# Second model's kernel on one core: paired matmuls in the feed-forward stages, GpSimd's share of low parts in the mixers, the order of the norm and of the first mixture's copies

## The chip, the cores and the metric

The kernel runs on one core of a Trainium2 chip. The metric is the device time of one execution in microseconds, the median of several runs; less is better. The engines are TensorE (PE in the profile, its weight loads PEld), VectorE (DVE), ScalarE (ACT), GpSimd (POOL) and SyncE (SP, which issues the loads of weights).

## The reference

One batch of 256 tokens, 1024 wide, goes through two chained models, all in float32:

```python
def first_block(x, mem, ...):            # two layers
    for layer in range(2):
        if layer == 0: mix = gla_layer_mixer(h, mem, ...)   # gated linear attention + memory attention
        else:          mix = sb_layer_mixer(h, mem, ...)    # stick-breaking attention + memory attention
        h = layer_norm(ALPHA * h + mix)
        h = layer_norm(ALPHA * h + peer(h, ...))            # 16384 experts, top 16 in each of 8 heads
    return h

def gla_layer_mixer(x, ...):
    q, k, v, r, glr, qm = jnp.split(x @ w_in, A_IN_SPLITS, axis=-1)
    log_g = log_sigmoid(glr @ w_gate2 + b_gate) / 16
    o = gla_chunked(q * 64 ** -0.5, k, v, log_g)            # 6 heads, chunks of 64 tokens
    o = o * rsqrt(mean(o * o) + EPS) * head_g
    o = o * silu(r)
    return concatenate([o, memory_attention(qm, mem, w_mem_kv)]) @ w_out

def second_block(x, ...):                # two layers
    for l in range(2):
        x = x + 0.5 * swiglu(rms_norm(x), w_gate, w_up, w_down)      # (silu(h wg) * (h wu)) wd, 2816 wide
        na, df, gq, dl = split(rms_norm(x) @ w_in)          # 4 heads each, with norms and rotations
        o = [neighborhood(na), diff(df), gqa_axial(gq), dilated(dl)]  # diff: (p0 - lam * p1) v, then rms_norm
        x = x + concatenate(o) @ w_out
        x = x + 0.5 * swiglu(rms_norm(x), w_gate, w_up, w_down)
```

## The kernel before

**Products.** Every weight is read once from memory, as 933 units of 512 KB, in the order of use. A unit has two halves of 128 x 512; a half is split into a high part WH (rounded to the fast float32 form, ScalarE, `split`, L1152) and a low part WL = RAW - WH (VectorE at L1758, or GpSimd at L2562 where `low_on_pool(j)` says so: every fourth half, j % 4 == 3, but for some stretches). Activations are split likewise, XTh and XTl. A product is three matmuls: high x high, low x high, high x low, all recorded at L475 (`mm`). The halves pass through five slots (NHALF), the raw units through four (NRAW). ScalarE makes the high part of half j + 5 once TensorE has used half j (`spent`).

**Two forms of product.** In `Tensor.cols` (L498) the weights are the stationary operand and 256 tokens move: 12 matmuls of 256 columns for a half. In `Tensor.depth` (L555) the activations stand, the weights move, 512 columns in each matmul, 2 blocks of tokens x 3 = 6 matmuls for a half, summed in the banks 0 to 3.

**Stages.** Ten stages: gated linear attention (37 units), PEER (272), stick breaking (28), PEER (272), feed forward (66), mixer (30), feed forward, feed forward (66 each), mixer (30), feed forward (66). In the profile of before the first runs to about 159 us, the PEERs to 999 and from 1141 to 1982, the first mixer of the second model from 2186 to 2346, the second from 2732 to 2892.

**Feed forward.** 22 steps over f: gate and up (`cols`, two halves each, both in one bank, 4 + f % 4, gate in its first 256 columns and up in its last), then the product of hidden unit f - 2 (`depth`). The hidden chain of f runs beside it: VectorE multiplies the gate part by the norm's factor (GR, L2408), ScalarE takes Silu (L1620), VectorE multiplies by up (HID, L2412), ScalarE makes the high part FH (L1624), VectorE the low part FL (L2414).

**The order around it.** Each engine's program is written out by one Python class (Tensor, Scalar, Vector, Gpsimd, Sync) with the same stage functions. What does not belong to the stream of halves is a generator in a `Pace`: each half is one `tick`, which adds `rate` to a credit and steps the background list `bg` while there is credit, and each generator of the foreground list `fg` once. `until(name)` steps until a name is reached, foreground first. In a mixer the background is the four attentions (na, df, gq, dl), and between df and gq the norm of difference attention, `od`. The queues are in order on each engine: a background instruction stands where the ticks put it. ScalarE's `halves(n)` does n ticks with a `split` behind each; the copy of a finished bank out of PSUM comes behind that (L1420, L1430 in the first mixture, L1486 in stick breaking, L1544 in PEER). Attention: VectorE's row maximum of a head (L1994), ScalarE's exponentials (L1291), transposes on TensorE, ScalarE's copy of them (L1300), products with the values, VectorE's output (L2022 and others). L2485 to L2490 with L1777 to L1790 are VectorE's part of `od`, L2451 and L2457 the norms of the queries and keys, L2500 and L1681 copies out of the input product, L2434 to L2440 rotations, L1976 the low part of the output product's activations.

## Time and profile before

| | before |
|---|---|
| median of three runs | 3088.6 us (3087.66 to 3089.96) |
| the profiled execution | 3092.74 us, of it 3090.5 us span |
| TensorE matmul | 3000.8 us (97%), 21828 instructions |
| VectorE | 2109.8 us (68%) |
| ScalarE | 1628.2 us (53%) |
| GpSimd | 469.1 us (15%), 363 instructions |
| TensorE's mean granted clock | 0.983 of full |

The span is the time from the first to the last recorded instruction of the profiled execution; its own time is 2.24 us longer. A matmul's row shows its start exactly and its end by a model, so the time that one costs in a stream is the distance to the next start, not its length. The idle time ahead of an instruction stands in brackets, with what ended it. The granted clock says which share of the full 2.4 GHz TensorE had in a stretch: 0.50 is 1.2 GHz.

### The profile page before, as it was taken

To read this page: it belongs to the slowest core of one execution; us is meant where nothing else is said; L and a number is where in the kernel's file an instruction comes from. 1 tells how busy PE (TensorE), PEld (TensorE's weight loads), DVE (VectorE), ACT (ScalarE), POOL (GpSimd) and SP (SyncE) were. 2 spreads that over 40 slices of the span, in tenths; PEclk is the share of its full clock that TensorE was granted. 3 is DMA by queue.
4 is the path that set the end of the run, shared out by engine and by line. 5 is a ranking of instruction groups with operands and counts; after the bars stand their busy time and mean duration, and the time that the engine had idled before them with its cause. 6 is when DMAs were issued, how large, how long until landed. Compare 5 with 4: busy or idle time off the path is not lost.

```text
span 3090.5 us, 56441 instructions
## 1 busy us (share of the span) xinstructions
PE 3000.8 (97%) x21828; PEld 2712.4 (88%) x21828; DVE 2109.8 (68%) x4512; ACT 1628.2 (53%) x3157; POOL 469.1 (15%) x363
## 2 busy tenths in 40 slices
PE   8989999999999989999999999899989999998999
PEld 8789999988887879999998888799868999987898
DVE  4559978799755555997879965655765565566555
ACT  5445544454555555554444455555655555565554
POOL 1212200000022112220000012123101222311122
PEclk9999999999999999999999999999999999999999
DMA  6345554454555335554454555465423556542354
GB/s 216 121 144 182 181 175 161 158 170 164 191 191 177 127 100 174 178 186 163 160 166 163 167 198 191 153 219 185 152 75 132 189 176 214 185 162 76 130 184 157
DMA packets 138363, 509.47 MB, mean 165 GB/s; under 512 B 15329, under 2 KB 15858, under 8 KB 136818
## 3 DMA queue, kind: packets, MB, share of 16 engines
q1 hardware_dynamic: 134352, 489.22, 48.0%
q10 hardware_dynamic: 3746, 16.65, 1.5%
q8 instruction: 174, 2.85, 0.4%
q14 instruction: 91, 0.75, 0.1%
HBM read 504.76 MB, written 1.05 MB: 164 GB/s over the span
## 4 chain that ended last, share of the span: by engine, by line
PE 89%; DVE 6%; ACT 3%; issue 1%; DMA 0%; POOL 0%; ACTq 0%; DVEq 0%
PE ps L475 88%; PE ps L479 1%; ACT WH L1152 1%; DVE WL L1758 1%; ACT BIG L1291 1%; DVE XTl L1830 0%; DVE BIG L1994 0%; DVE BIG L1799 0%; DVE BIG L2500 0%; DVE BIG L1847 0%; DMA BIG<-in_memT 0%; DVE BIG L1989 0%; DVE BIG L2451 0%; DVE H L1924 0%; DVE BIG L1855 0%
## 5 line engine op out<-in xcount | busy, mean ns | idle before, releaser
L1152 ACT ACTIVATE WH<-RAW 128x512 fp32r<-128x512 f32 x1866 | 1158.4, 630 | 1082.1 <-PE ps L475 1068.7
L1758 DVE TENSOR_TENSOR WL<-RAW,WH 128x512 fp32r<-128x512 f32 x1537 | 1102.7, 725 | 710.1 <-ACT WH L1152 698.8
L475 PE MATMUL ps<-XTh,WH 128*128 128x256 f32 x3928 | 1128.4, 287 | 19.8 <-DVE XTl L1807 8.7
L475 PE MATMUL ps<-XTl,WH 128*128 128x256 f32 x3928 | 1118.4, 285 | 0.0
L475 PE MATMUL ps<-XTh,WL 128*128 128x256 f32 x3928 | 1118.0, 285 | 0.0
L2562 POOL TENSOR_TENSOR WL<-RAW,WH 128x512 fp32r<-128x512 f32 x329 | 440.5, 1339 | 2593.6 <-ACT WH L1152 2593.6
L475 PEld LDWEIGHTS ps<-XTh,WH 128*128 128x128 f32 x3928 | 760.2, 194 | 28.6 <-issue 9.8
L475 PEld LDWEIGHTS ps<-XTl,WH 128*128 128x128 f32 x3928 | 760.8, 194 | 2.9
L475 PEld LDWEIGHTS ps<-XTh,WL 128*128 128x128 f32 x3928 | 760.2, 194 | 0.0
L475 PE MATMUL ps<-WH,GH 128*128 128x512 f32 x1056 | 420.2, 398 | 6.5 <-DVE BIG L2435 2.0
L475 PE MATMUL ps<-WH,GL 128*128 128x512 f32 x1056 | 413.7, 392 | 0.0
L475 PE MATMUL ps<-WL,GH 128*128 128x512 f32 x1056 | 413.5, 392 | 0.0
L475 PEld LDWEIGHTS ps<-WH,GH 128*128 128x128 f32 x1056 | 199.0, 188 | 48.0 <-issue 6.2
L475 PEld LDWEIGHTS ps<-WH,GL 128*128 128x128 f32 x1056 | 199.3, 189 | 42.1
L475 PE MATMUL ps<-WH,HIDR 128*128 128x512 f32 x704 | 233.8, 392 | 1.2 <-POOL WL L2562 1.2
L475 PEld LDWEIGHTS ps<-WL,GH 128*128 128x128 f32 x1056 | 199.4, 189 | 39.1
L475 PE MATMUL ps<-BIG 128*128 128x64 f32 (+6 forms) x966 | 157.3, 313 | 16.9 <-ACT BIG L1291 8.2
L475 PEld LDWEIGHTS ps<-BIG 128*128 128x128 f32 (+4 forms) x966 | 126.8, 192 | 43.2 <-issue 12.8
L475 PE MATMUL ps<-WH,XTh 128*128 128x512 f32 (+1 forms) x400 | 158.4, 396 | 1.1 <-ACT BIG L1420 1.1
L475 PEld LDWEIGHTS ps<-WH,HIDR 128*128 128x128 f32 x704 | 132.6, 188 | 29.1 <-POOL WL L2562 2.9
L475 PE MATMUL ps<-WH,XTl 128*128 128x512 f32 (+1 forms) x400 | 150.0, 375 | 0.0
L475 PE MATMUL ps<-WL,XTh 128*128 128x512 f32 (+1 forms) x400 | 149.6, 374 | 0.0
(197 smaller groups left out, 2590.7 us busy)
## 6 DMA issues: line engine op xcount, KB each, us to landing
RAW<-in_w SPq DMA_DIRECT2D x933, 512.0 KB, 3.3
BIG<-in_ln ACTq DMA_DIRECT2D x4, 1024.0 KB, 7.8
BIG<-in_sk ACTq DMA_DIRECT2D x2, 1024.0 KB, 5.1
BIG<-in_na_bias ACTq DMA_DIRECT2D x2, 1024.0 KB, 5.0
BIG<-in_qk_gain ACTq DMA_DIRECT2D x2, 960.0 KB, 5.8
BIG<-in_memT ACTq DMA_DIRECT2D x4, 256.0 KB, 7.6
BIG<-in_xT ACTq DMA_DIRECT2D x1, 1024.0 KB, 5.3
H<-in_x ACTq DMA_DIRECT2D x1, 1024.0 KB, 8.1
```

The source lines that it names most:

```text
L475: return self.e.matmul(out, lhsT, rhs, start=start, stop=stop, skip_group_check=loose)
L479: return self.e.transpose(out, in_, self.c.IDENT[0:n, 0:n])
L1152: e.activation(wh, raw, ACT.Copy).then_inc(*c.hi.mark(j))
L1291: e.activation(t.E[:, i % 3, w], src[:, w], ACT.Exp, bias=s[:, blk:blk + 1], accum_out=s[:, 2 + blk:3 + blk]).then_inc(*c.exps.mark(tag, i ...
L1758: e.tensor_tensor(wl, raw, wh.bitcast(F32), ALU.subtract).then_inc(*c.lo_v.mark(j))
L2562: e.tensor_tensor(wl, raw, wh.bitcast(F32), ALU.subtract).then_inc(*c.lo_p.mark(j))
```

## The change

It has six parts.

1. `low_on_pool`: inside a mixer, from the 16th half to four before the end, every second half's low part is GpSimd's, not every fourth.
2. The norm `od` is appended to the foreground when difference attention is done, no longer an item of the background between df and gq; `until` takes the background first unless it is `od` that is wanted; chunk 2 of the output product waits for it.
3. XTh and XTl are the halves of one tile XT of 512 columns. Gate and up of f from 2 on are made by `wide_cols`: WH by [XTh | XTl] in one matmul of 512 columns, WL by XTh in one of 256. The two parts of the result stand beside each other and have to be added: ScalarE copies the second (PARTS), VectorE adds it. Gate and up have a bank each, 6 and 7 or 4 and 5 in turn.
4. `depth`, where it starts a sum, takes token block 1 first and waits for each bank apart, no longer for all four ahead.
5. ScalarE's `halves` takes a function for the copy of the finished bank, and issues it ahead of the last tick and high part.
6. The first mixture: the scores of a pair of heads wait for that pair's q and k alone; the root of each pair's norm is taken by itself; the first gating is made early; the Silu of the gate is taken in the copy out of PSUM, with its table loaded ahead.

```diff
+    if any(BASE[stage] + 16 <= j < BASE[stage + 1] - 4 for stage in MIX):
+        return j % 2 == 1
     return j % 4 == 3
...
     def until(self, name):
         while name not in self.reached:
-            q = self.fg or self.bg
+            q = self.bg if self.bg and name[1] != "od" else self.fg or self.bg
             self.step(q[0], q)
...
+        self.XT = sb("XT", [P, 8, 512], FR)
+        self.XTh, self.XTl = self.XT[:, :, 0:256], self.XT[:, :, 256:512]
...
+    def wide_cols(self, key, ps):
+        c = self.c
+        for half in range(2):
+            j, wh, wl = self.half(key)
+            parts = blocks(4)
+            for a in range(4):
+                self.mm(ps[:, :], wh[:, parts[a]], c.XT[:, half * 4 + a, :], half + a == 0, half * 4 + a == 7, loose=True)
+            for a in range(4):
+                t = self.mm(ps[:, 0:256], wl[:, parts[a]], c.XTh[:, half * 4 + a, :], False, half * 4 + a == 7, loose=True)
+            t.then_inc(*c.used.mark(j))
+            self.pace.tick()
...
     def depth(self, key, ah, al, first):
-            for blk in range(2):
-                t = self.three(c.B[blk * 2 + half][:, :], ah[:, TB[blk]], al[:, TB[blk]], wh, wl, first, False)
+            for blk in (1, 0) if first else (0, 1):
+                out = c.B[blk * 2 + half]
+                if first:
+                    out = self.bank(blk * 2 + half)
+                t = self.three(out[:, :], ah[:, TB[blk]], al[:, TB[blk]], wh, wl, first, False)
...
     def inner(self):                       # Tensor, first mixture
         for p in range(3):
-            e.wait_ge(*c.vec.at("ke"))
+            e.wait_ge(*c.vec.at("qe", p))
...
     def ffn_stage(self, layer, which):     # Tensor
-            ps = self.bank(4 + f % 4)
-            self.cols(("fg", layer, which, f), ps[:, 0:256], stage if f == 0 else None)
-            self.cols(("fu", layer, which, f), ps[:, 256:512])
-            self.empty[4 + f % 4] = c.vec.at(stage, "hid", f)
+            if f < 2:
+                ps = self.bank(4 + f)
+                self.cols(("fg", layer, which, f), ps[:, 0:256], stage if f == 0 else None)
+                self.cols(("fu", layer, which, f), ps[:, 256:512])
+                self.empty[4 + f] = c.vec.at(stage, "hid", f)
+            else:
+                for b, key in zip((6, 7) if f % 2 == 0 else (4, 5), ("fg", "fu")):
+                    self.wide_cols((key, layer, which, f), self.bank(b))
+                    self.empty[b] = c.vec.at(stage, "hid", f)
...
     def halves(self, n, done=None):        # Scalar
-        for _ in range(n):
+        for k in range(n):
             self.j += 1
+            if done and k == n - 1:
+                self.e.wait_ge(*self.c.used.at(self.j - 1))
+                done()
             self.pace.tick()
             self.split()
...
     def hidden(f):                         # Scalar
+            if f >= 2:
+                for k, ps in enumerate(c.ffn_banks(f)):
+                    e.wait_ge(*c.used.at(BASE[stage] + 4 * f + 2 * (f - 2) + 1 + 2 * k))
+                    if f >= 4:
+                        e.wait_ge(*c.vec.at(stage, "hid", f - 2))
+                    e.activation(t.PARTS[:, 2 * r + k, :], ps[:, 256:512], ACT.Copy).then_inc(*c.act.mark(stage, "parts", f, k))
...
     def hidden(f):                         # Vector
+                e.wait_ge(*c.act.at(stage, "parts", f, 0))
+                e.tensor_tensor(t.GR[:, r, :], gate[:, 0:256], t.PARTS[:, 2 * r, :], ALU.add).then_inc(*c.vec.mark())
+                self.own()
+                e.tensor_tensor(t.GR[:, r, :], t.GR[:, r, :], c.RB, ALU.mult).then_inc(*c.vec.mark(stage, "gr", f))
+                e.wait_ge(*c.act.at(stage, "parts", f, 1))
+                e.tensor_tensor(t.UP[:, r, :], up[:, 0:256], t.PARTS[:, 2 * r + 1, :], ALU.add).then_inc(*c.vec.mark("up", stage, f))
+                up = t.UP[:, r, :]
+                self.own()
...
     def attend(self, stage, name, k):      # and on each other engine
         yield from self.attention(...)
+        if name == "df":
+            self.pace.fg.append(self.od(stage))
...
     def gla_stage(self):                   # Scalar
-        e.wait_ge(*c.vec.at("sum", 2))
-        self.rsqrt(t.rs[:, 0:12], 1.0 / 128, c.EPS5, ..., "rsum")
-        e.activation(t.vr[:, :, 1024:1536], t.vr[:, :, 1024:1536], ACT.Silu).then_inc(*c.act.mark("silu", 1))
         e.preload_act_table_set(TABLES)
+        self.gla_root(2)
```

TensorE in a feed-forward stage of the second model, one half of gate, up and the hidden product, before. ps6 and so on are the PSUM banks, HIDR holds the hidden unit's parts:

```order
L475 MATMUL ps6<-XTh,WH 128x256
L475 MATMUL ps6<-XTl,WH 128x256
L475 MATMUL ps6<-XTh,WL 128x256
L475 MATMUL ps6<-XTh,WH 128x256
L475 MATMUL ps6<-XTl,WH 128x256
L475 MATMUL ps6<-XTh,WL 128x256
L475 MATMUL ps0<-WH,HIDR 128x512
L475 MATMUL ps0<-WL,HIDR 128x512
L475 MATMUL ps0<-WH,HIDR 128x512
L475 MATMUL ps2<-WH,HIDR 128x512
L475 MATMUL ps2<-WL,HIDR 128x512
L475 MATMUL ps2<-WH,HIDR 128x512
```

The same place, changed, from gate and up of one f to the hidden product:

```order
L486 MATMUL ps6<-XT,WH 128x512 x4
L486 MATMUL ps6<-XT,WL 128x256 x4
L486 MATMUL ps6<-XT,WH 128x512 x4
L486 MATMUL ps6<-XT,WL 128x256 x4
L486 MATMUL ps7<-XT,WH 128x512 x4
L486 MATMUL ps7<-XT,WL 128x256 x4
L486 MATMUL ps7<-XT,WH 128x512 x4
L486 MATMUL ps7<-XT,WL 128x256 x4
L486 MATMUL ps2<-WH,HIDR 128x512
L486 MATMUL ps2<-WL,HIDR 128x512
```

A triple of 256 columns has become a matmul of 512 columns and one of 256; the low parts WL now come last in a half, gate and up stand in two banks.

VectorE in the first mixer of the second model, behind the input product's last copies (L2500), before. ps4 and ps5 are the scores of two heads:

```order
L2500 SCALAR_TENSOR_TENSOR BIG<-ps1,BIG 128x512
L2485 TENSOR_REDUCE BIG<-BIG 128x8
L1777 TENSOR_SCALAR BIG<-BIG,CST 128x8
L1784 TENSOR_TENSOR BIG<-BIG 128x8
L1786 TENSOR_TENSOR BIG<-BIG 128x8
L1788 TENSOR_SCALAR BIG<-BIG 128x8
L1790 TENSOR_TENSOR BIG<-BIG 128x8
L2490 TENSOR_TENSOR BIG<-BIG 128x2x256
L2451 TENSOR_REDUCE BIG<-BIG 128x16
L1976 TENSOR_TENSOR GL<-ps6,GH 128x512
L1994 TENSOR_REDUCE BIG<-ps4 128x2
L1994 TENSOR_REDUCE BIG<-ps5 128x2
```

Changed (L2576 is L2500, L2041 is L1994, L2560 is L2485, L2524 is L2451):

```order
L2576 SCALAR_TENSOR_TENSOR BIG<-ps1,BIG 128x512
L2041 TENSOR_REDUCE BIG<-ps4 128x2
L2041 TENSOR_REDUCE BIG<-ps5 128x2
L2524 TENSOR_REDUCE BIG<-BIG 128x16
L2023 TENSOR_TENSOR GL<-ps6,GH 128x512
L2560 TENSOR_REDUCE BIG<-BIG 128x8
L1824 TENSOR_SCALAR BIG<-BIG,CST 128x8
L2041 TENSOR_REDUCE BIG<-ps4 128x2
L2041 TENSOR_REDUCE BIG<-ps5 128x2
```

The two maxima stood behind the norm and the reduction L2451; now they come first, and the norm is spread behind them.

ScalarE at the end of the first mixture, before. ps0 and ps1 are the input product's last banks, L1170 and L1172 the norm's root, L1443 the gate's Silu:

```order
L1152 ACTIVATE WH<-RAW 128x512 x3
L1430 ACTIVATE BIG<-ps0 128x512
L1430 ACTIVATE BIG<-ps1 128x512
L1170 ACTIVATE BIG<-BIG,CST 128x12
L1172 ACTIVATE BIG<-BIG 128x12
L1443 ACT_TABLE_LOAD
L1443 ACTIVATE BIG<-BIG 128x2x512
L1444 ACT_TABLE_LOAD
L1152 ACTIVATE WH<-RAW 128x512 x2
```

Changed (L1471 is L1430, L1179 is L1152, L1201 and L1203 are the root of the last pair):

```order
L1422 ACT_TABLE_LOAD
L1422 ACTIVATE BIG<-CST 128x1
L1309 ACTIVATE GH<-ps6 128x512
L1179 ACTIVATE WH<-RAW 128x512 x2
L1471 ACTIVATE BIG<-ps0 128x512
L1471 ACTIVATE BIG<-ps1 128x512
L1179 ACTIVATE WH<-RAW 128x512
L1485 ACT_TABLE_LOAD
L1201 ACTIVATE BIG<-BIG,CST 128x4
L1203 ACTIVATE BIG<-BIG 128x4
L1179 ACTIVATE WH<-RAW 128x512 x2
```

The Silu table is loaded ahead, the pass over 1024 columns is gone, and the copies of ps0 and ps1 come behind two high parts instead of three.

## Rows read from the trace of the kernel before

**Rows 1.** The page: busy us and share of an engine; the chain that ended last.

```profile
PE 3000.8 (97%) x21828; PEld 2712.4 (88%) x21828; DVE 2109.8 (68%) x4512; ACT 1628.2 (53%) x3157; POOL 469.1 (15%) x363
...
PE 89%; DVE 6%; ACT 3%; issue 1%; DMA 0%; POOL 0%; ACTq 0%; DVEq 0%
```

**Rows 2.** Table by windows: length, busy us of each engine (count), granted clock, DMA.

```profile
2186.00:2346.00 160.00, 147.12 (x766) 117.11 (x765) 99.29 (x224) 87.98 (x226) 19.08 (x14) 0.95 0.29 99
2354.00:2531.00 177.00, 176.69 (x1266) 167.01 (x1265) 99.36 (x173) 93.52 (x175) 40.11 (x32) 1.00 0.56 184
```

**Rows 3.** Timeline of TensorE, feed forward: start, length, [idle before <-what ended it].

```profile
2018.20 0.28 PE L475 MATMUL ps<-XTh,WH 128*128 128x256 f32 x1
...
2023.96 0.40 PE L475 MATMUL ps<-WH,HIDR 128*128 128x512 f32 x1
...
2026.70 0.28 PE L475 MATMUL ps<-XTh,WH 128*128 128x256 f32 x1
```

**Rows 4.** Timeline of VectorE, feed forward, the hidden chain.

```profile
2455.89 0.42 DVE L2408 TENSOR_TENSOR BIG<-ps,BIG 128x256 f32<-128x256 f32 x1
2456.85 0.42 DVE L2412 TENSOR_TENSOR BIG<-BIG,ps 128x256 f32<-128x256 f32 x1 [0.55 <-ACT BIG L1620]
```

**Rows 5.** Timeline of ScalarE, the same stretch.

```profile
2457.31 0.42 ACT L1624 ACTIVATE HIDR<-BIG 128x256 fp32r<-128x256 f32 x1 [0.56 <-DVE BIG L2412]
2457.63 1.73 ACT L1152 ACTIVATE WH<-RAW 128x512 fp32r<-128x512 f32 x3
```

**Rows 6.** Timeline of GpSimd, the same stretch.

```profile
2458.33 1.30 POOL L2562 TENSOR_TENSOR WL<-RAW,WH 128x512 fp32r<-128x512 f32 x1 [6.09 <-ACT WH L1152]
```

**Rows 7.** Timeline of TensorE, the same stretch: the low part's first use.

```profile
2461.65 0.28 PE L475 MATMUL ps<-XTh,WL 128*128 128x256 f32 x1
```

**Rows 8.** The tile RAW: duration of its readers in ns, min/median/max.

```profile
L1758 DVE TENSOR_TENSOR WL<-RAW,WH x1537: 661/692/1787, 6.3 to 3080.7; 128x512 fp32r<-128x512 f32 x193
...
L2562 POOL TENSOR_TENSOR WL<-RAW,WH x329: 1265/1297/2277, 11.2 to 3076.3; 128x512 fp32r<-128x512 f32 x165
```

**Rows 9.** Timeline of VectorE, first mixer of the second model.

```profile
2281.95 1.40 DVE L2500 SCALAR_TENSOR_TENSOR BIG<-ps,BIG 128x512 f32<-128x512 f32 x2
2283.27 0.67 DVE L2485 TENSOR_REDUCE BIG<-BIG 128x8 f32<-128x512 f32 x1
...
2287.70 1.28 DVE L1994 TENSOR_REDUCE BIG<-ps 128x2 f32<-128x512 f32 x2
```

**Rows 10.** Timeline of TensorE, first mixer of the second model.

```profile
2283.61 1.99 PE L475 MATMUL ps<-BIG 64*128 64x256 f32 x8
2289.48 2.07 PE L475 MATMUL ps<-BIG 64*128 64x256 f32 x4 [3.88 <-ACT BIG L1291]
...
2302.03 0.70 PE L475 MATMUL ps<-WH,GH 128*128 128x512 f32 x1 [0.98 <-DVE BIG L2435]
```

**Rows 11.** Timeline of ScalarE, the same stretch.

```profile
2288.41 0.47 ACT L1291 ACTIVATE BIG<-ps,BIG 128x256 f32<-128x256 f32 x1 [2.89 <-DVE BIG L1994]
```

**Rows 12.** TensorE's waits, 2186 to 2346: us in total, times, longest.

```profile
PE ps L479 <- ACT BIG L1300: 3.7, 4, 2.2
```

**Rows 13.** Table by windows as in rows 2, of stretches at half clock.

```profile
134.60:138.00 3.40, 3.40 (x9) 2.54 (x9) 1.79 (x5) 3.36 (x4) 0.00 (x0) 0.51 0.47 154
2288.50:2295.30 6.80, 5.82 (x21) 4.65 (x21) 2.60 (x8) 3.79 (x16) 0.00 (x0) 0.50 0.18 68
```

**Rows 14.** Timelines of TensorE in the first model: first mixture, PEER, stick breaking.

```profile
76.98 0.50 PE L475 MATMUL ps<-WH,XTh 128*128 128x512 f32 x1 [1.05 <-ACT BIG L1420]
...
106.55 1.53 PE L475 MATMUL ps<-BIG 64*128 64x256 f32 x6 [0.44 <-issue]
...
133.65 0.47 PE L475 MATMUL ps<-WH,GH 128*128 128x512 f32 x1 [1.90 <-ACT BIG L1170]
...
220.13 3.06 PE L475 MATMUL ps<-BIG 128*128 128x128 f32 x25 [1.05 <-ACT BIG L1544]
...
1109.19 0.47 PE L475 MATMUL ps<-WH,GH 128*128 128x512 f32 x1 [1.52 <-ACT BIG L1486]
```

149 lines of the change are left out of this document (84 added, 65 removed).

## The prediction, made before the change was run

> **What bounds the kernel now.** I read the page's busy shares and its chain first. TensorE is busy 97% of the span, and 89% of the chain that ended last is TensorE [rows 1]: time is saved only where TensorE issues less, stops waiting, or gets its clock back. The table by stage comes next, to see where it is not full: a feed-forward stage fills 176.69 of 177 us of its steady part, a mixer 147.12 of 160 us at a granted clock of 0.95 [rows 2]. So a feed-forward stage can be shortened by cheaper matmuls alone, a mixer by its waits.
>
> In the feed-forward stage I read the starts of TensorE's rows, since ends are modelled. From the first product with XTh at 2018.20 to the first hidden product at 2023.96 lie 48 matmuls of 256 columns, 0.120 us each; from there to 2026.70 lie 12 of 512 columns, 0.228 us each [rows 3]. One iteration over f is 5.76 + 2.74 = 8.50 us.
>
> **The change part by part.**
>
> *Paired matmuls.* A half now costs 12 × 0.120 = 1.44 us. Changed, it is 4 matmuls of 512 columns and 4 of 256: 4 × 0.228 + 4 × 0.120 = 1.392 us, 0.048 less. Halves of gate and up with f of at least 2: 4 × 20 × 4 stages = 320. That is **−15.4 us**. A pitch of 0.226 would make it −17.9, one of 0.230 −12.8; I take 0.228, since it is measured beside the 256-column stream itself. These columns are charged at full clock, where the stages run [rows 2].
>
> TensorE's saving is only real if nothing else becomes late. ScalarE gains two copies of 256 columns in each f, VectorE two additions. Today the hidden unit's chain runs: gate × RB on VectorE at 2455.89, product at 2456.85 [rows 4], high part on ScalarE at 2457.31, and only then three high parts of weights at 2457.63, which had queued behind it [rows 5]. The first of them feeds the GpSimd low part at 2458.33, done at 2459.63 [rows 6]; the half that uses it sends its first low product at 2461.65 [rows 7]. The slack is 2.0 us. The chain grows by VectorE's addition ahead of gate × RB (0.42 us), and by what the second copy pushes the Silu back, about as much: some 0.8 us. That is within the slack, and the new order of a half gives 0.9 us more, since its low products come behind four matmuls of 512 columns. Cost taken: 0. Its cover is those 2.0 us; the bound above them is rival D. Below nothing it cannot go: no wait stands in this place to be won.
>
> The banks of gate and up are used again two iterations later instead of four; the product that frees them runs at 2456.85 [rows 4], some 0.8 us later then, and their next use is over 8 us behind that: nothing waits there.
>
> *Pool's share.* The order gives GpSimd ten more low parts in each mixer, and VectorE ten fewer. On VectorE that is 10 × 0.692 = 6.9 us less, on GpSimd 10 × 1.297 = 13.0 us more [rows 8]. For a waiting product a GpSimd low comes 0.6 us later than VectorE's, and NHALF = 5 slots of lead cover that, as they did in the half above (2.0 us). In the queue of VectorE, which is what the attentions wait for, it is a gain, but one that is spread. I put it at 0 by itself, ±1 us for each mixer.
>
> The same medians have a tail: VectorE's low takes up to 1.787 us and GpSimd's up to 2.277 [rows 8]. The Trainium skill, page "SBUF — State Buffer", section "🔬 SBUF: two separate sides", says that GpSimd and a VectorE operation with two SBUF inputs take their shared port as an exclusive lock, so that the other fully blocks; the tails agree with it. By that rule the ten moved lows per mixer could give back as much VectorE time as they free, and the sum would lose what the mixers gain; this is rival E.
>
> *Norm of difference attention, and the order in the queues.* Ahead of TensorE's longest wait in the mixer, ScalarE's exponentials wait for VectorE's two maxima at 2287.70. Those stand behind the norm (L2485 at 2283.27 and what follows it) and another reduction (L2451), which come right behind the two of L2500 [rows 9]. TensorE makes the scores from 2283.61 on, and next does something at 2289.48, 3.88 us idle [rows 10]. In the changed order both maxima follow the two copies of L2500, and the norm comes behind them. The scores of the first head are four of eight matmuls in 1.99 us, so there at 2284.6; maximum 0.64 us to 2285.3; two exponentials, 1.07 us as now (2288.41 [rows 11] to 2289.48): TensorE goes on at about 2286.4, 3.0 us earlier. What is late next is the same chain for the later heads, and the first output product at 2302.03, which waits 0.98 us on VectorE [rows 10]. Less VectorE work ahead of it gives another 1 us. **−4 us for each mixer, −8 us.** The wait of chunk 2 of the output product for the norm costs nothing: the norm's last step is done tens of instructions ahead of it. Bounds: −1 (the gap only moves to the waits on L1300, now 3.7 us in four [rows 12]) and −10 (below).
>
> *The clock.* Behind each long gap comes a stretch at half clock: 2288.5 to 2295.3 runs at 0.50, TensorE busy for 5.82 of 6.80 us [rows 13], so it holds some 3 us that could be saved. I take no gain of it, because waits like those on L1300 (the longest 2.2 us) remain.
>
> *First mixture (GLA).* ScalarE's copy of a finished bank comes ahead of the next high part instead of behind it (0.58 us each: three in 1.73 [rows 5]): of TensorE's 1.05 us at 76.98 some 0.5 goes. Scores need one pair of q and k, not all three: of the idle time ahead of 106.55 (0.44, and the matmul's slow start) up to 0.6. The gap of 1.90 us at 133.65 [rows 14] is the two copies of 512 columns plus one high part ahead of them; bank by bank, and with the roots and the first gating done earlier, it goes: −2.0, the start of its first matmul with it. The half-clock stretch behind it (134.6 to 138.0, TensorE busy in all of 3.40 us [rows 13]) would go with the gap: −1.7. Sum **−4.8 us**; at worst nothing, if the gating on VectorE is late in its place. ScalarE loads as many tables as before.
>
> *The other copies.* Stick-breaking mixer, 1.52 us at 1109.19: the last bank's copy comes ahead of a high part and long before the gap: −1.5. Query stage of PEER, 1.05 at 220.13: −0.5, twice [rows 14]. **−2.6 us.**
>
> **Sum.** −15.4 − 8 − 4.8 − 2.6 = −30.8 us. Against the profiled execution's own 3092.74 us (span 3090.5 and 2.24 around it) that is 3061.9. This execution is 4.1 above the median of the three, 3088.6, so for the median I say **3057.8 us**.
>
> **Rivals.**
>
> *B, the pair saves nothing.* If a matmul is charged by columns alone, a 512-column one costs two of 256, 0.240 us, and 15.4 us of the sum go: 3073.2 us. For it: the columns streamed are the same. Against it: 0.228 stands in the trace beside 0.120 [rows 3]. The Trainium skill, page "TensorE: Matmul & The Clock Gate", section "Back-to-back issue gap", gives an isolated gap of N/2.4 + 2.5 ns, by which a pair saves only 2.5 ns, or an estimated 3.2 us over 1280 pairs; the trace's pitch of 0.120 us for 256 columns differs from it, and the measurement decides.
>
> *C, the mixers' half-clock stretches go too.* With the gap of 3.88 us closed, two of the stretches [rows 13] fall away, 3 us each, in both mixers: −12 more, 3045.8 us. For it: the stretches begin only behind gaps. Against it: the waits on L1300 stay.
>
> *D, slower: the longer hidden chain takes all slack.* VectorE waits in order for ScalarE's copies, and ScalarE's high parts are queued behind the Silu. If all four added operations lie in series, with two handshakes of 0.55 us as ahead of the product [rows 4], the chain grows by 4 × 0.42 + 2 × 0.55 = 2.8 us; less the 2.0 of slack TensorE waits 0.8 us in each of 80 iterations, +64 us: 3122 us. It decides from a growth of 2.0 us on, and eats the whole gain from 2.4 us. Against it: the first copy runs beside the up product's matmuls and the up addition beside the Silu.
>
> *E, the ten moved lows collide.* A colliding low costs VectorE up to 1.1 us more (1.787 against 0.692), so ten of them free nothing, and the mixers' queues are as late as now: the 8 us go, 3065.8 us. For it: the tails [rows 8], and mixers whose VectorE works on SBUF alone in long operations. Against it: only 14 GpSimd operations in 160 us today [rows 2].
>
> *F, the change does little of what it says,* the gaps in first mixture, mixers and PEER being set by something else, and the pairs eaten by waits: about 3086 us. The order shows the pairs and the moved maxima, so this is small.
>
> **How the numbers follow.** Forecast A 0.55, B 0.10, C 0.18, D 0.04, E 0.09, F 0.04. Two tenths of a per cent, 6.2 us, is what a measurement of this kernel can tell from no change. A, B, C and E are faster: 0.92; F the same: 0.04; D slower: 0.04. The range reaches down to C with a pair's upper bound (3045.8 − 2.5, some rounding down: 3042), and up to B, or to A without the mixers' 8, the first mixture's 4.8 and 2.6 of the pairs (3073.2): 3074. D and F are left out, and the tails of the others.
>
> **What would show it.** In the changed profile: 512-column products of XT and WH starting 0.228 us apart and an iteration of 8.31 us (8.50 − 4 × 0.048); TensorE busy in all of a feed-forward stage, its waits under 1 us each; ScalarE's high parts queued behind the hidden chain no later than 2.0 us. A mixer with the gap of 3.88 us down to about 1 and 156 us long; half clock still in two or three stretches. No gap at the start of the first mixture's output product. The prediction is wrong if high or low parts of weights release TensorE in the feed-forward stages (D), if pairs start 0.240 apart (B), or if mixers keep 160 us.

## The result and the profile after

The changed kernel takes 3069.2 us, the median of six runs (3065.61 to 3071.44), against 3088.13 (3087.41 to 3089.96) for the kernel before: 18.9 us less, a ratio of 0.9936 with a 95% interval of 0.9924 to 0.9949. Forecast were 3057.8 us within 3042 to 3074. The sign and the range held; of the 30.8 us that the sum promised, 12 did not come.

The page of the changed kernel, its busy times and its chain, answers to [rows 1]. Lines have moved: L486 is L475, L1179 is L1152, L1805 is L1758, L2637 is L2562.

```profile
PE 2984.5 (97%) x20548; PEld 2637.2 (86%) x20548; DVE 2183.1 (71%) x4666; ACT 1666.0 (54%) x3321; POOL 499.2 (16%) x383
...
PE 87%; DVE 7%; ACT 4%; issue 1%; DMA 0%; POOL 0%; ACTq 0%; DVEq 0%
```

There are 1280 matmuls fewer, 20 operations more on GpSimd, 154 more on VectorE, and TensorE still bounds the whole: its share of the chain fell by 2 points, VectorE's and ScalarE's rose by one each.

The table by windows of the changed kernel, one row for each stage, cut at TensorE's last product of the stage (length, TensorE's busy us, granted clock, DMA share, GB/s):

```profile
0.00:161.30 161.30, 146.90 (x852) 0.99 0.48 165
161.30:1000.50 839.20, 830.23 (x6615) 0.99 0.54 174
1000.50:1140.50 140.00, 130.21 (x865) 0.95 0.35 115
1140.50:1980.10 839.60, 831.10 (x6615) 0.99 0.54 174
1980.10:2182.30 202.20, 191.78 (x1028) 0.97 0.56 185
2182.30:2337.50 155.20, 145.25 (x768) 0.97 0.32 102
2337.50:2528.80 191.30, 189.09 (x1020) 0.99 0.56 182
2528.80:2720.20 191.40, 189.12 (x1019) 0.99 0.59 195
2720.20:2874.60 154.40, 143.68 (x767) 0.98 0.31 103
2874.60:3063.60 189.00, 186.83 (x1012) 1.00 0.55 173
```

The same cuts in both traces, in us, with the time that each stage spent at half clock (the cuts are read to 0.01 us here and rounded, so a length can differ by 0.1 from a row's):

| stage | before | after | difference | forecast | half clock before, after |
|---|---|---|---|---|---|
| first mixture | 158.9 | 161.3 | +2.4 | -4.8 | 3.4, 3.4 |
| PEER | 840.2 | 839.2 | -1.0 | -0.5 | 13.7, 10.2 |
| stick breaking | 141.9 | 140.0 | -1.9 | -1.5 | 13.7, 13.7 |
| PEER | 840.6 | 839.6 | -1.0 | -0.5 | 13.7, 13.7 |
| feed forward | 204.2 | 202.2 | -2.0 | -3.85 | 13.7, 13.7 |
| mixer | 160.5 | 155.2 | -5.3 | -4 | 17.1, 10.2 |
| feed forward | 193.3 | 191.3 | -2.0 | -3.85 | 3.4, 3.4 |
| feed forward | 191.9 | 191.4 | -0.5 | -3.85 | 0, 3.4 |
| mixer | 160.7 | 154.4 | -6.3 | -4 | 17.1, 6.8 |
| feed forward | 192.4 | 188.9 | -3.5 | -3.85 | 3.4, 0 |

The differences sum to -21.1 us, as do the spans (3090.5 to 3069.4). Two places are off: the pairs gave half of what was forecast, and the first mixture became longer. The mixers gave 3.6 us more. The profiled execution took 3071.28 us, 2.1 above the median of the six, and its mixers hold more half clock than others of the same code: in a kernel below whose mixers are not edited (the gating behind the pair's low part) they take 153.2 and 153.8 us, with 3.4 us at half clock in each.

**The pairs, in the trace.** TensorE's timeline of the changed kernel in a feed-forward stage, one iteration from its first product with XT to the hidden product:

```profile
2447.01 1.07 PE L486 MATMUL ps<-XT,WH 128*128 128x512 f32 x4
2447.92 0.64 PE L486 MATMUL ps<-XT,WL 128*128 128x256 f32 x4
2448.39 1.09 PE L486 MATMUL ps<-XT,WH 128*128 128x512 f32 x4
2449.32 0.63 PE L486 MATMUL ps<-XT,WL 128*128 128x256 f32 x4
...
2452.60 0.40 PE L486 MATMUL ps<-WH,HIDR 128*128 128x512 f32 x1
```

Four of 512 columns take 0.91 to 0.93 us from the first start to the next group's (0.2325 each in the second and later halves, not 0.228), four of 256 take 0.47 (0.118, not 0.120). The four halves take 2452.60 - 2447.01 = 5.59 us, against 5.76 [rows 3]. The hidden product's twelve take 2.77 us on the mean of this stage, against 2.74. An iteration is 8.35 us long, not the 8.31 of the forecast, and was 8.50: 0.15 saved, 0.19 forecast.

The hidden chain, VectorE and then ScalarE, answers to [rows 4, 5]. L2475 and L2479 are the two additions, L2477 the product with the norm's factor, L2485 the hidden unit, L1661 the two copies:

```profile
2445.78 0.42 DVE L2475 TENSOR_TENSOR BIG<-ps,BIG 128x256 f32<-128x256 f32 x1
2446.23 0.42 DVE L2477 TENSOR_TENSOR BIG<-BIG 128x256 f32<-128x256 f32 x1
2446.57 0.42 DVE L2479 TENSOR_TENSOR BIG<-ps,BIG 128x256 f32<-128x256 f32 x1
2447.24 0.43 DVE L2485 TENSOR_TENSOR BIG<-BIG 128x256 f32<-128x256 f32 x1 [0.25 <-ACT BIG L1665]
```

```profile
2445.04 0.64 ACT L1661 ACTIVATE BIG<-ps 128x256 f32<-128x256 f32 x2
...
2448.02 1.66 ACT L1179 ACTIVATE WH<-RAW 128x512 fp32r<-128x512 f32 x3
```

and GpSimd, which answers to [rows 6]:

```profile
2448.71 1.30 POOL L2637 TENSOR_TENSOR WL<-RAW,WH 128x512 fp32r<-128x512 f32 x1 [5.95 <-ACT WH L1179]
```

Counted from the start of the hidden product (2454.35 before, 2444.24 now), HID starts 3.0 us behind it where it was 2.5, and the three queued high parts start at 3.78 where they were at 3.28: the chain grew by 0.5 us. That is inside the slack of 2.0: the GpSimd low behind the first of them is done at 2450.01, and TensorE first uses it at 2452.13, 2.1 us later. TensorE waits nowhere in the steady iterations.

**The mixer, in the trace.** VectorE and then TensorE of the changed kernel, answering to [rows 9, 10]; L2576 is L2500, L2041 is L1994, the maxima:

```profile
2279.52 1.41 DVE L2576 SCALAR_TENSOR_TENSOR BIG<-ps,BIG 128x512 f32<-128x512 f32 x2
2280.84 1.28 DVE L2041 TENSOR_REDUCE BIG<-ps 128x2 f32<-128x512 f32 x2
```

```profile
2279.30 1.99 PE L486 MATMUL ps<-BIG 64*128 64x256 f32 x8
...
2283.24 1.13 PE L486 MATMUL ps<-BIG 64*128 64x256 f32 x4
...
2291.36 0.66 PE L490 MATMUL ps<-CST,BIG 128*128 128x128 f32 x4 [1.29 <-ACT BIG L1331]
...
2296.65 0.47 PE L486 MATMUL ps<-WH,GH 128*128 128x512 f32 x1 [0.48 <-ACT BIG L1735]
```

From the first scores to the output product were 2302.03 - 2283.61 = 18.4 us; now 2296.65 - 2279.30 = 17.35. From the first scores to the third head's were 5.87, now 3.94; the idle 3.88 us ahead of it are gone. These two distances understate the gain, because the changed order puts other products there: TensorE makes 96 matmuls between the first scores and the output product, where it made 68. The 69th of them starts 18.4 us behind the first before and 13.0 us now. What was late next is ScalarE's copy of transposes (1.29 us at 2291.36). The output product runs its first six matmuls at full clock, where they were at half: they start 0.23 us apart, not 0.43.

### The profile page after: what moved, and what is told of

The parts are those of the page before. It is cut to its first block, busy times and chain, and to the rows that moved or that the text cites. A ratio compares the mean times of both kernels' runs of the same rounds, so it can differ in the third digit from the quotient of the medians.

```text
span 3069.4 us, 54436 instructions
## 1 busy us (share of the span) xinstructions
PE 2984.5 (97%) x20548; PEld 2637.2 (86%) x20548; DVE 2183.1 (71%) x4666; ACT 1666.0 (54%) x3321; POOL 499.2 (16%) x383
## 3 DMA queue, kind: packets, MB, share of 16 engines
HBM read 504.76 MB, written 1.05 MB: 165 GB/s over the span
## 4 chain that ended last, share of the span: by engine, by line
PE 87%; DVE 7%; ACT 4%; issue 1%; DMA 0%; POOL 0%; ACTq 0%; DVEq 0%
PE ps L486 86%; PE ps L490 1%; ACT WH L1179 1%; DVE WL L1805 1%; ACT BIG L1322 1%; DVE BIG L2041 0%; DVE XT L1877 0%; DVE BIG L1846 0%; DVE BIG L2576 0%; DVE BIG L1894 0%; DMA BIG<-in_memT 0%; DVE BIG L2036 0%; DVE BIG L2530 0%; DVE BIG L2485 0%; DVE H L1971 0%
## 5 line engine op out<-in xcount | busy, mean ns | idle before, releaser
L1179 ACT ACTIVATE WH<-RAW 128x512 fp32r<-128x512 f32 x1866 | 1152.4, 629 | 998.2 <-PE ps L486 986.9
L1805 DVE TENSOR_TENSOR WL<-RAW,WH 128x512 fp32r<-128x512 f32 x1517 | 1100.8, 735 | 647.4 <-ACT WH L1179 639.0
L486 PE MATMUL ps<-XT,WH 128*128 128x256 f32 (+1 forms) x6576 | 1327.7, 308 | 20.2 <-DVE XT L1854 8.7
L486 PEld LDWEIGHTS ps<-XT,WH 128*128 128x128 f32 x6576 | 1059.1, 193 | 60.8 <-issue 9.9
L486 PE MATMUL ps<-XT,WL 128*128 128x256 f32 x3928 | 957.6, 283 | 0.0
L2637 POOL TENSOR_TENSOR WL<-RAW,WH 128x512 fp32r<-128x512 f32 x349 | 470.1, 1347 | 2538.7 <-ACT WH L1179 2538.7
L486 PEld LDWEIGHTS ps<-XT,WL 128*128 128x128 f32 x3928 | 710.0, 192 | 26.8
L486 PE MATMUL ps<-WH,GH 128*128 128x512 f32 x1056 | 418.9, 397 | 2.6 <-DVE GL L2412 1.0
L486 PE MATMUL ps<-WH,GL 128*128 128x512 f32 x1056 | 411.8, 390 | 0.0
L486 PE MATMUL ps<-WL,GH 128*128 128x512 f32 x1056 | 411.6, 390 | 0.0
L486 PE MATMUL ps<-WH,XT 128*128 128x512 f32 (+1 forms) x800 | 255.3, 386 | 3.9 <-DVE XT L2023 3.4
L486 PE MATMUL ps<-WH,HIDR 128*128 128x512 f32 x704 | 236.0, 395 | 2.2 <-POOL WL L2637 1.8
L486 PEld LDWEIGHTS ps<-WH,GH 128*128 128x128 f32 x1056 | 198.3, 188 | 44.3 <-DVE GL L2412 2.8
L486 PEld LDWEIGHTS ps<-WH,GL 128*128 128x128 f32 x1056 | 198.2, 188 | 42.1
L486 PEld LDWEIGHTS ps<-WL,GH 128*128 128x128 f32 x1056 | 198.6, 188 | 38.8
L486 PEld LDWEIGHTS ps<-WH,XT 128*128 128x128 f32 x800 | 148.9, 192 | 36.6 <-issue 8.0
L486 PE MATMUL ps<-BIG 128*128 128x64 f32 (+6 forms) x966 | 155.5, 311 | 8.0 <-DVE BIG L2258 2.1
L486 PEld LDWEIGHTS ps<-WH,HIDR 128*128 128x128 f32 x704 | 132.2, 188 | 32.4 <-POOL WL L2637 3.5
L486 PEld LDWEIGHTS ps<-BIG 128*128 128x128 f32 (+4 forms) x966 | 125.6, 191 | 33.3 <-issue 12.8
L486 PE MATMUL ps<-WL,XT 128*128 128x512 f32 (+1 forms) x400 | 149.7, 374 | 0.0
L486 PE MATMUL ps<-WL,HIDR 128*128 128x512 f32 x352 | 138.4, 393 | 0.0
L2412 DVE TENSOR_TENSOR GL<-BIG,GH 128x256 fp32r<-128x256 f32 x256 | 107.4, 420 | 0.2
```

The lines of the kernel that those rows point to most:

```text
L486: return self.e.matmul(out, lhsT, rhs, start=start, stop=stop, skip_group_check=loose)
L1179: e.activation(wh, raw, ACT.Copy).then_inc(*c.hi.mark(j))
L1805: e.tensor_tensor(wl, raw, wh.bitcast(F32), ALU.subtract).then_inc(*c.lo_v.mark(j))
L2412: e.tensor_tensor(c.GL[:, r, :], c.peer.G[:, g, :], c.GH[:, r, :].bitcast(F32), ALU.subtract).then_inc(*c.xtl.mark(stage, "g", g))
L2637: e.tensor_tensor(wl, raw, wh.bitcast(F32), ALU.subtract).then_inc(*c.lo_p.mark(j))
```

## Experiments

Each edit is to the changed kernel, unless it says otherwise. Comparisons with the kernel before are with its runs beside it, 3087.6 to 3090.2 us in the median.

### Pairs undone, and pairs alone

```diff
-                for b, key in zip((6, 7) if f % 2 == 0 else (4, 5), ("fg", "fu")):
-                    self.wide_cols((key, layer, which, f), self.bank(b))
+            self.cols(("fg", layer, which, f), ps[:, 0:256], stage if f == 0 else None)
+            self.cols(("fu", layer, which, f), ps[:, 256:512])
```

> The changed kernel with gate and up made by matmuls of 256 columns again, in one bank for each f, without the two copies and two additions of each hidden unit; all else as changed. Theory (the pairs save what the starts show, 8.50 us an iteration before and 8.35 changed, less 0.8 us of new waits in each feed-forward stage): this run is slower than the changed kernel by 80 x 0.15 - 4 x 0.8 = 9 us, about 3078 us, with iterations of 8.50 us. Rival B (columns are all that is paid, and the stages became shorter by the earlier copies and banks): within 2 us of the changed kernel.

Measured: 3074.4 us (3073.95 to 3078.94), ratio to before 0.9955 (0.9938 to 0.9972), 5.2 us slower than the changed kernel. Its feed-forward stages are those of the kernel before again: 204.2, 193.3, 192.0 and 192.5 us. Rival B is out. But 5.2 is less than the 9 of the theory, and the runs of either kernel spread by 5 us, much of it with the granted clock. The two executions of each kernel with a mean clock of 0.990 lie 8 us apart (3073.95 and 3073.96, against 3065.61 and 3066.22). The stages, below, give the same size.

The other way round, to the kernel before, the pairs and with them the waits bank by bank in `depth` (and in PEER, where four waits ahead of the sum go):

> The kernel before with the pairs alone: gate and up by matmuls of 512 and 256 columns with their copies, additions and banks, and the sum's banks waited for one by one. Theory: 0.147 us less for each of 80 iterations, 0.8 us of new waits in each of four stages: 8 to 9 us faster than before, 3079 to 3080 us. Rival (the gain needs the other parts, or what the table by stage shows is partly their work): 3084 us or more.

Measured: 3073.2 us (3071.02 to 3073.53), ratio 0.9948 (0.9932 to 0.9965), 14.8 us less than before, more than expected. The stages show why. Stick breaking is 1.7 us shorter and the mixers are 2.0 and 4.0 us shorter in this kernel, and none of them has a pair. In stick breaking that is `depth` starting its sum bank by bank: the 1.52 us ahead of the output product [rows 14] are gone from this trace, and stand unchanged in the one with the norm's order alone. In the mixers `depth` is the one edited part that they use, but half clock fell too, from 17.1 us to 13.7 and 10.2, and how the gain divides is not shown. A feed-forward stage without half clock is 189.9 us long here, 192.0 in the kernel without pairs. The row by windows of the third such stage, with the pairs alone:

```profile
2529.60:2719.60 190.00, 187.74 (x1020) 160.77 (x1019) 133.31 (x245) 114.94 (x248) 55.14 (x45) 1.00 0.61 197
```

and with the pairs undone:

```profile
2532.90:2724.80 191.90, 189.91 (x1339) 177.83 (x1338) 113.94 (x204) 105.35 (x207) 54.57 (x45) 1.00 0.60 195
```

So the pairs are worth 2.0 us in a stage, both at full clock, 8 in all. The steady iterations give 20 x 0.15 = 3.0 of it; 0.8 to 1.0 us go at the two ends of the stage, where the hidden chain has no slack: by the starts, some 0.15 us at the first hidden product, where TensorE waits 0.45 us on a GpSimd low instead of 0.30, 0.33 in the turn after it and 0.36 ahead of the last products.

### The order of lengths

```diff
             for a in range(4):
                 self.mm(ps[:, :], wh[:, parts[a]], c.XT[:, half * 4 + a, :], ...)
-            for a in range(4):
                 t = self.mm(ps[:, 0:256], wl[:, parts[a]], c.XTh[:, half * 4 + a, :], ...)
```

> The changed kernel with a half of gate and up in alternating order: WH by 512 columns, WL by 256, four times, no longer four of one and four of the other. The starts in the changed kernel are 0.232 us apart for 512 columns and 0.118 for 256, where I had 0.228 and 0.120. Theory A (the cost is one for each matmul, of whatever length, and the order of lengths does not matter): the iteration stays at 8.35 us and the time within 1 us. Theory B (runs of one length, or loads of weights that come nearer together in the 256-column run, cost something): the iteration falls to 8.31 us, 3 us less in all. Rival C (each change of length costs): 8.4 us or more, 4 us slower or worse.

Measured: 3066.3 us (3065.59 to 3068.31), no more than 3 us from the changed kernel, within both spreads. The trace is sharper. Two hidden products that follow each other start 8.39 us apart:

```profile
2442.20 0.40 PE L486 MATMUL ps<-WH,HIDR 128*128 128x512 f32 x1
...
2450.59 0.40 PE L486 MATMUL ps<-WH,HIDR 128*128 128x512 f32 x1
```

and the two stages without half clock take 190.4 and 190.5 us, where the next kernel below has 189.8 and 189.9. A half has eight changes of length, not two, and costs 0.01 us more. Theories A and B are wrong. Rival C is right in kind, that changes of length cost, and wrong in its price of 4 us: the iterations sum to some 3 us, and the whole shows none of it. In this order a 512-column matmul starts 0.236 us ahead of its successor, a 256-column one 0.117 (medians). What makes the pitch of one depend on its neighbours stays open.

### GpSimd's share in the mixers

```diff
-    if any(BASE[stage] + 16 <= j < BASE[stage + 1] - 4 for stage in MIX):
-        return j % 2 == 1
```

> The changed kernel with the old rule for GpSimd's low parts (every fourth half) in the mixers of the second model; all else as changed. Theory (most of the 5.3 and 6.3 us that a mixer gained come from the order of the maxima and the norm): the mixers lose about 1 us each and the run is 1 to 3 us slower than the changed kernel. Rival (freeing VectorE of ten low parts made the gain): a mixer is 4 us longer, the run 8 us slower. Rival E (moved lows collide and give back what they free): no difference or faster by 1 to 2 us.

Measured: 3067.1 us (3063.12 to 3073.01), ratio 0.9931 (0.9914 to 0.9948). The mixers by windows (TensorE, its loads, VectorE, ScalarE, GpSimd):

```profile
2183.40:2337.50 154.10, 144.12 (x767) 114.46 (x766) 100.82 (x226) 88.20 (x227) 18.82 (x14) 0.98 0.32 103
2717.20:2871.70 154.50, 145.24 (x768) 115.39 (x767) 100.26 (x226) 88.28 (x228) 18.79 (x14) 0.97 0.32 103
```

In the changed kernel, with the larger share:

```profile
2182.30:2337.50 155.20, 145.25 (x768) 115.26 (x766) 95.85 (x216) 88.22 (x227) 33.35 (x24) 0.97 0.32 102
2720.20:2874.60 154.40, 143.68 (x767) 114.51 (x766) 96.41 (x216) 88.19 (x227) 33.29 (x24) 0.98 0.31 103
```

GpSimd's larger share takes 5.0 and 3.9 us off VectorE and nothing off the stage; neither the theory's 1 us nor the rival's 4 us for each mixer came. The ten lows alone took 6.7 us off VectorE. Its 179 other operations are the same in both kernels, and with the larger share they take 1.3 and 2.5 us longer in sum (79.4 against 78.1, and 80.1 against 77.6): the three products of 1024 columns in the first mixer take 1.59 us on the mean, not 1.22. That is rival E's collision, at a part of its price.

### The norm's place

```diff
+        pace.bg.insert(2, self.od(stage, layer))
...
-        if name == "df":
-            self.pace.fg.append(self.od(stage, layer))
```

> The changed kernel with the norm of difference attention back in the background between df and gq, and the old rule of what a wait for a name steps first; all else as changed, GpSimd's share too. Theory (the order of the maxima is the gain): the gap of 3.9 us ahead of the first scores of gq is back, with its half clock, and each mixer is 4 to 5 us longer: 8 to 10 us slower than the changed kernel. Rival (GpSimd's share is the gain): within 2 us of it.

Measured: 3076.9 us (3075.39 to 3079.54), ratio 0.9966 (0.9953 to 0.9978), 7.7 us slower than the changed kernel; the mixers take 158.9 and 158.4 us. The gap is back, in TensorE's timeline:

```profile
2284.32 2.07 PE L485 MATMUL ps<-BIG 64*128 64x256 f32 x4 [3.90 <-ACT BIG L1320]
```

And alone, put into the kernel before:

> The kernel before with the norm of difference attention in the foreground and the new rule of waiting for a name, nothing else. Theory: the maxima come ahead of the norm, the gap of 3.9 us ahead of the scores closes, and each mixer is 4.5 us shorter plus what half clock goes with it, 9 to 12 us in all: 3077 to 3080 us. Rival (it works only with the ten lows moved to GpSimd): under 5 us.

Measured: 3075.7 us (3073.24 to 3079.28), ratio 0.9958 (0.9944 to 0.9972), 12.3 us less than before. Each mixer is 153.8 us long, 6.8 less, at a clock of 0.99:

```profile
2185.90:2339.80 153.90, 142.61 (x768) 112.84 (x766) 100.85 (x227) 88.42 (x228) 18.73 (x14) 0.99 0.32 103
```

The order alone gives the whole gain in the mixers, with GpSimd's old share. By the same count of matmuls in both traces, this kernel is 4.3 us ahead directly behind where the gap stood, 5.9 us ahead 60 matmuls later and 6.7 to 6.9 at the stage's end; half clock fell from 17.1 us to 3.4 in each mixer. The gains do not add: the pairs' kernel, with `depth` bank by bank, gave 2.0 and 4.0, the norm alone 6.7 and 6.9, both together 5.3 and 6.3 in the profiled execution, with 10.2 and 6.8 us of half clock, and 7.4 and 6.9 in the one with 3.4 us in each. So what all other parts add in the mixers once the norm is moved is 0.7 us at most.

### The first mixture

The changed trace shows the stage 1.5 us ahead of the kernel before at its output product (132.15 against 133.65 [rows 14]) and 2.4 us behind at its end. That it is longer is no accident of one execution: in the five traces whose first mixture is the changed kernel's (this one and the runs without pairs, with a quarter for GpSimd, with the norm in the back and alternating) it ends at 159.7 to 162.0 us, in the two whose first mixture is that of the kernel before at 158.9. From the output product's first start to its last are 29.0 to 30.4 us in the five and 25.3 in the two. TensorE waits inside the product:

```profile
132.15 0.50 PE L486 MATMUL ps<-WH,GH 128*128 128x512 f32 x1 [0.56 <-DVE GL L2023]
137.46 0.50 PE L486 MATMUL ps<-WH,GH 128*128 128x512 f32 x1 [0.34 <-DVE WL L1805]
142.50 0.55 PE L486 MATMUL ps<-WH,XT 128*128 128x512 f32 x1 [3.38 <-DVE XT L2023]
```

VectorE's queue up to the low part of XT that it waits for (L1831 to L1837 are a root's last steps, L2178 and L2182 the gating of the next pair):

```profile
137.94 1.25 DVE L1831 TENSOR_TENSOR BIG<-BIG 128x4 f32<-128x4 f32 x1
...
139.82 0.69 DVE L2178 TENSOR_TENSOR BIG<-BIG 128x512 f32<-128x512 f32 x1
140.55 0.69 DVE L2182 TENSOR_TENSOR BIG<-BIG 128x512 f32<-128x512 f32 x1
...
141.76 0.68 DVE L2023 TENSOR_TENSOR XT<-ps,XT 128x512 fp32r<-128x512 f32 x1
```

and GpSimd beside it:

```profile
137.31 1.86 POOL L2637 TENSOR_TENSOR WL<-RAW,WH 128x512 fp32r<-128x512 f32 x1 [0.52 <-ACT WH L1179]
```

ScalarE's high part of that XT was there at 138.2. Three things stand between: an operation on four columns that takes 1.25 us, where its like takes 0.16, and ends when GpSimd's low does (139.19 and 139.17); the root's steps; and the next pair's gating. First the order:

```diff
         def early(ch):
-            if ch < 4:
-                self.gla_root(ch // 2 + 1)
-                self.gated_heads(ch // 2 + 1)
+            if ch > 0:
+                self.gla_root(ch // 2)
+                self.gated_heads(ch // 2)
```

> The changed kernel with one thing moved on VectorE: in the first mixture the root and the gating of heads 2 and 3 (and then 4 and 5) come behind the low part of the pair before them, as in the kernel before; the first gating stays early. Theory (the gap of 3.4 us on TensorE ahead of the first product with XT at 142.5 is VectorE's order, the low part of XT waits behind the next gating): the gap shrinks to under 1 us, the half clock behind it goes, and the run is 3 to 5 us faster than the changed kernel, 3064 to 3066 us. Rival (the roots pair by pair themselves, with a handshake for each, are what is late): the gap moves to the next pair and the time stays within 1 us.

Measured: 3067.8 us (3066.3 to 3071.16), 1.4 us from the changed kernel, within the spread. The first mixture ends at 161.1 us, not 161.3. What the rival foretold came: the wait moved.

```profile
140.24 0.50 PE L486 MATMUL ps<-WH,XT 128*128 128x512 f32 x1 [1.26 <-DVE XT L2023]
144.53 0.66 PE L490 MATMUL ps<-CST,BIG 128*128 128x128 f32 x4 [1.27 <-DVE BIG L2182]
152.65 0.66 PE L490 MATMUL ps<-CST,BIG 128*128 128x128 f32 x4 [2.00 <-DVE BIG L2182]
```

Now each gating is waited for, and one operation of each lies beside a GpSimd low (the second one runs from 150.05 to 151.33):

```profile
142.82 1.65 DVE L2182 TENSOR_TENSOR BIG<-BIG 128x512 f32<-128x512 f32 x1
...
150.10 1.77 DVE L2178 TENSOR_TENSOR BIG<-BIG 128x512 f32<-128x512 f32 x1
```

```profile
142.65 1.28 POOL L2637 TENSOR_TENSOR WL<-RAW,WH 128x512 fp32r<-128x512 f32 x1 [3.61 <-ACT WH L1179]
```

So the lows were taken from GpSimd, to that order:

```diff
-    return j % 4 == 3
+    return j % 4 == 3 and j not in (63, 67, 71)
```

> The run with the gating behind the pair's low part, and three lows of the first mixture's output product (the 16th to 18th that GpSimd makes) on VectorE. Theory (what lengthened the output product from 23.4 to some 27.5 us is, beside the order, VectorE operations of 0.16 and 0.69 us that last 1.25 to 1.77 us while a GpSimd low runs, and four small root operations of 0.75 us ahead of each gating): without the GpSimd lows the gatings last 0.69 us each and the product is 2 us shorter, 25 to 26 us, though VectorE has three lows more. Rival (VectorE is simply full there, collisions or not): no shorter than with the gating moved alone.

Measured: 3067.3 us (3064.75 to 3068.82); the output product takes 26.6 us, where it took 29.1 (from the first matmul's start to the last's; 25.3 in the kernel before). The theory had 25 to 26. The rival is out: VectorE has three lows more and the product is shorter all the same. The roots' place instead, GpSimd's lows kept:

```diff
+            if ch > 0:
+                self.gated_heads(ch // 2)
             if ch < 4:
                 self.gla_root(ch // 2 + 1)
-                self.gated_heads(ch // 2 + 1)
```

> The run with the gating behind the pair's low part, and each root's four small operations one place earlier, behind the gating before it, ahead of the pair's low part; GpSimd's lows as changed. Theory: the gatings of the second and third pair no longer have 0.75 us ahead of them, the waits of TensorE on the gating (1.27 and 2.00 us) shrink by 0.75 each, 1 to 1.5 us off the output product. Rival (the first low part is late by as much): the wait ahead of the first product with XT grows by 0.75 and takes half of it back.

Measured: 3067.2 us (3064.51 to 3069.92); the product takes 26.4 us, 2.7 less, more than the 1 to 1.5 expected: with the four small steps elsewhere the gatings are through (144.11) as the GpSimd low begins (144.03), and it is a root's step that meets it now. VectorE:

```profile
142.69 0.69 DVE L2178 TENSOR_TENSOR BIG<-BIG 128x512 f32<-128x512 f32 x1
143.42 0.69 DVE L2182 TENSOR_TENSOR BIG<-BIG 128x512 f32<-128x512 f32 x1
144.21 1.13 DVE L1831 TENSOR_TENSOR BIG<-BIG 128x4 f32<-128x4 f32 x1
```

The rival is seen as well: TensorE waits 1.9 us ahead of the first product with XT, where it waited 1.26. Both:

> Both of the two together. Theory: the output product of the first mixture takes 23.5 to 24.5 us, as long as in the kernel before, and since it starts about 2 us earlier the first mixture ends near 157 us; the whole 3 to 4 us under the changed kernel, 3065 us. Rival: the product stays above 26 us, and its length comes from something else.

Measured: 3065.7 us (3064.13 to 3067.8), ratio 0.9922 (0.9906 to 0.9939). The product takes 25.9 us, the stage ends at 158.5. The two cures share what they cure; 24.5 was not reached, since 1.4 us are still waited for ahead of XT. The 23.4 us that the expectations give for the kernel before are 25.3 by this measure, so the product is 0.6 us longer than there, not 2.5. With the second root behind the first pair's low part:

```diff
+            if ch == 2:
+                self.gla_root(1)
             if ch > 0:
                 self.gated_heads(ch // 2)
+            if ch == 2:
+                self.gla_root(2)
```

> The run with roots and lows together, with the second root's four small operations behind the first pair's low part, no longer ahead of it: in the first mixture's output product VectorE does low part of pair 0, root 1, gating 1, root 2, low part of pair 1, gating 2, and has the three lows that GpSimd had. Theory: the wait of 1.5 us ahead of the first product with XT loses 0.75, none comes elsewhere, the output product takes 25 us from its first matmul and the whole 3064 to 3066 us, 3 to 5 us under the changed kernel. Rival (the second gating is now late by as much): no shorter than with the root ahead, 3065 to 3067 us.

Measured: 3063.0 us (3062.55 to 3065.18, five runs), ratio 0.9919 (0.9906 to 0.9933). That is 6.2 us under the changed kernel, with spreads that do not meet, though its first mixture is only 3.0 us shorter (158.3 us, output product 25.7); the rest is where half clock fell in the mixers and the stages behind them, which this edit does not touch. Against the changed kernel's two executions at a clock of 0.990, 3065.6 and 3066.2, it is about 3 us. Even so repaired, the first mixture ends only 0.7 us ahead of the kernel before (158.95). TensorE's waits in the product:

```profile
140.23 0.50 PE L486 MATMUL ps<-WH,XT 128*128 128x512 f32 x1 [0.76 <-DVE XT L2023]
143.56 0.65 PE L490 MATMUL ps<-CST,BIG 128*128 128x128 f32 x4 [0.30 <-DVE BIG L2182]
```

Last, the whole of the first mixture's part undone, but for the copies ahead of the high part:

> The changed kernel with its part 6 undone: scores wait for all keys, one root of 12 columns behind all sums, no early gating, the gate's Silu as a pass of its own, but the finished bank's copy still ahead of the high part. Theory (the roots pair by pair and the gatings in the output product's queue cost more than the earlier start gives): the first mixture ends near 158 us, not 161.3, and the whole is 2 to 4 us faster than the changed kernel, 3066 us. Rival: as in the changed kernel or slower, since the gap of 1.9 us ahead of the output product and its half clock are back.

Measured: 3071.2 us (3067.56 to 3073.02), not faster: the stage ends at 160.9 us. The output product is short (26.6 us), but TensorE waits 1.9 us at the first scores, which wait for all keys, where the kernel before waited nothing. Two things make the keys late. ScalarE's high part stands behind the copy now, and VectorE's low and its three products of keys with it: the first of these starts at 77.92, not 77.30. And the last of them, 128 x 768, took 2.02 us, where its two predecessors took 0.95, beside a GpSimd low at 79.21 of 1.65:

```profile
79.65 2.02 DVE L2109 TENSOR_TENSOR BIG<-BIG 128x768 f32<-128x768 f32 x1
```

So the scores pair by pair, which need not wait for that product, are worth their place beside the copies; it is the roots pair by pair and the gating ahead of a needed low part that cost.

## Why the prediction was right in sign and short by 12 us

- **TensorE bounds all; a feed-forward stage by its matmuls, a mixer by its waits.** Right, in all traces.
- **The pairs, -15.4 us.** Rival B was wrong, forecast A right in kind, its term too large: -8. Two sizes were off. The step "I take 0.228, since it is measured beside the 256-column stream" took a pitch from a stream of 512 columns for one in which lengths alternate; there it is 0.2325, and the saving 0.15 us an iteration, -12 us, which is outside the bounds of -12.8 to -17.9 by a little. And the step "cost taken: 0", right for the steady iterations, was not made for the first and last ones, where the hidden chain has no slack: +3.4 to 4.
- **The hidden chain.** The growth was put at 0.8 us and measured 0.5; the slack of 2.0 held. Of the 0.9 us that the new order of a half was to add, 0.67 are right, since the first low product stood 0.24 us behind the half's start in the old order too. Rival D did not come, except for what is lost at the stages' ends.
- **GpSimd's share, 0.** Right: within about a microsecond in both mixers. Rival E's mechanism is real, as the times of VectorE show (4.4 us freed where 6.9 were moved), but it took back a third of what was freed, not all, and decided nothing there.
- **The norm, -8 us.** Mechanism and place right, size low: -11.6 in the mixers. The gap of 3.88 us closed, 3.0 of it expected; on top came 7 to 10 us less of half clock in each mixer. "I take no gain of it" was the wrong choice. "Less VectorE work ahead of it gives another 1 us" is not seen: with GpSimd's old share the mixers are as long. Rival C had the mechanism of the clock, at 6 us more in each mixer; measured were 1.3 and 2.3 more in the profiled execution of the changed kernel, 2.8 with the norm alone.
- **First mixture, -4.8 us.** Wrong: +2.4. The step that failed is "at worst nothing, if the gating on VectorE is late in its place". The start of the output product was looked at (it did come 1.5 us earlier), what is queued ahead of the next pair's low part was not: the root's steps and a gating more, and lows of GpSimd in whose time VectorE stands still. Only ScalarE's order was read for this term, and the wait stands on VectorE's. The -1.7 for the clock did not come either: the half clock of 3.4 us moved behind the new wait of 3.38 us.
- **Copies ahead of the high part, -2.6.** Its parts (1.5 and twice 0.5) sum to 2.5. Measured were -3.9 in the two PEER stages and stick breaking, but mostly by another cause. Nearly all of stick breaking's is `depth` bank by bank, which the sum had at nothing: 1.7 us with the pairs alone, where no copy was moved. Of the second PEER's 1.05 us 0.6 came there too, which leaves the 0.5 of the forecast to the copies; the first PEER had 3.4 us less of half clock as well.

## What to carry over

When an engine's work is moved earlier, list what then stands ahead of every operation that another engine waits for on that queue, not only ahead of the one the move is for. Price a matmul's pitch from a stream with the same mix of lengths, and a steady state's slack for its first and last turns apart. A norm or another long reduction belongs behind the row maxima of the next attention, not ahead of them.

## What the runs showed of the hardware

- A VectorE product, sum or difference of two SBUF tiles stands still while GpSimd subtracts 128 x 512 from one tile to another, however small it is: four columns took 1.25 us and ended with GpSimd's (139.19 and 139.17), 512 columns 1.65 and 1.77, 768 columns 2.02, against 0.16, 0.69 and 0.95 alone. Operations that read a single SBUF tile, or one beside PSUM, run on: in the changed kernel's trace a TENSOR_TENSOR of 128 columns with one input in PSUM (L2069) took 0.29 us in the seven cases that began with over 0.7 us of a GpSimd low to go, and 0.29 elsewhere, a MAX8 of 128 columns (L2286) 0.28 both ways, and a TENSOR_SCALAR with one tile as input (L1835) 0.15 both ways. So it is the form of the operation that decides whether a low moved to GpSimd costs VectorE anything. The Trainium skill, page "SBUF — State Buffer", section "🔬 SBUF: two separate sides", has this as an exclusive lock for an operation with two SBUF inputs; the traces agree. What is added to VectorE's operation is GpSimd's remaining time less some 0.15 us (1.09 us of 1.23 for the four columns, 1.08 of 1.23 for the 512).
- A 256-column matmul in this stream starts 0.120 us ahead of the next among its like, 0.118 in runs of four, 0.117 alternating; a 512-column one 0.228, 0.2325 and 0.236. A half of gate or up costs 1.44 us by 256 columns, 1.40 in runs of four and four, 1.41 alternating. By the pitches of streams of one length it would have been 1.39. Why the pitch depends on the neighbours stays open.
- Executions of one kernel differ by where half clock falls: of the changed kernel's six, the three with a mean granted clock of 0.987 took 3070.4 to 3071.4 us, the three with 0.989 or 0.990 took 3065.6 to 3068.0.
